# Tile 0's gate branch and projections first, tile 1's and the samples' between tile 0's expert rows

## The chip, the cores and the metric

One core of a Trainium2 chip runs the kernel. The metric is the device time of one execution in microseconds (us). TensorE (PE) multiplies matrices, VectorE (DVE), ScalarE (ACT) and GpSimd (POOL) do the rest, SyncE (SP) issues transfers, and 16 DMA engines move data between HBM and SBUF. PSUM, where TensorE writes, has 8 banks of 512 columns.

## The reference

One layer of a hybrid decoder over 256 prompt tokens and 8 sample tokens that share the weights, all in float32 with a model width D of 2048:

```python
h = rms_norm(x, norm1_w)
zb, zc, zx, zq, zk, zv, zmq, zg = jnp.split(h @ w_in, SPLIT_POINTS, axis=-1)
y_conv = (zb * short_conv(zc * zx)) @ w_conv_out
y_diff = rms_norm(diff_attn(q, k, v), subln_w) * (1 - lam_init) @ w_diff_out
y_mem  = mem_attn(qm, mem_k, mem_v) @ w_cross_out
g = sigmoid(zg.reshape(B, T, 3, D))
x = x + (g[:,:,0] * y_conv + g[:,:,1] * y_diff + g[:,:,2] * y_mem) @ w_o
# then experts: 8 heads, each token picks 16 of 16384 in every head
h2 = rms_norm(x, norm2_w);  q = (h2 @ w_peer_q).reshape(n, 8, 2, 128)
s1, s2 = q[:, :, 0] @ sub_keys[0].T, q[:, :, 1] @ sub_keys[1].T
idx, top_s = top_16_of_pair_sums(top_k(s1, 16), top_k(s2, 16))
a = einsum(take(peer_u, idx), h2);  w = softmax(top_s) * gelu(a)
x = x + einsum(w, take(peer_v, idx))
```

Every token reads 128 rows of `peer_u` and 128 of `peer_v`, each 8 KB, at places that only the scores tell.

## The kernel before

Tokens are three tiles: prompt tile 0 (128 tokens), prompt tile 1 (128) and the 8 samples, NT = 264 columns together. Activations lie turned, with features on the partitions: `hT` holds 16 blocks (KC) of 128 features by 264 tokens.

**Projections.** A weight matrix comes in blocks of 256 columns, [128, 16, 256] of float32, 2 MB, in runs of 1 KB, by SyncE into one of two buffers `wring[r]`. A block is two chunks. `chunk` (L569 to L574) adds 16 matmuls of a 128x128 piece of the weights (the stationary side) with 264 moving columns; each of these matmuls is two MATMUL and two LDWEIGHTS instructions in the trace. `linear` (L576) walks over the blocks. For w_o and w_peer_q a second step per chunk follows: `turner` (L589) turns w_o's chunk back to rows and VectorE adds it to x (L1256), `score` (L851) multiplies w_peer_q's chunk with the sub-keys. SyncE's `stream` fetches the next block into a buffer as soon as both chunks of the last one are done.

**Gate branches.** `gate_chunk` (L647) computes one unit: 16 matmuls for the gate's 128 columns (L651) and 8 for the branch's output (L663), whose weights come in 1 MB blocks to `bwring`, a part of `bregion`. ScalarE takes the sigmoid, VectorE multiplies and adds to `merged`. There are 48 units, q = 0 to 47, in three branches; the attention is threaded into the first 32 of them. The last 16 (`branch(2, ...)`, w_diff_out) stand alone.

**Experts.** Once the scores of a head are there, VectorE's `route` finds the 16 winners of each token and signals `idx_ready`. GpSimd then gathers: `gather_u` (one row of `peer_u` for each of 128 tokens, one indirect transfer of 1 MB) and `gather_v` (the same of `peer_v`). VectorE's `dot` (L1765) multiplies a gathered u row with `h2` and sums it. ScalarE makes a diagonal matrix of weights (L1150), and TensorE's `add_rows` (L878) adds diagonal x v row to four PSUM banks. A group g is one head of one tile, 16 slots: g 0 to 7 are tile 0's, g 8 to 15 tile 1's; the samples' 8 u rows are slots of their own inside g 7 and 8, and their v rows follow tile 0's. u rows have 4 buffers (`u_slots`), v rows 8 (`e_slots`). `v_before(n)` says how many v rows are gathered by u slot n: v follows u at a distance of 28 slots (`V_LEAD`).

**What sets the order.** Each engine runs its program in order and waits on counters. SyncE's stream, GpSimd's gathers, TensorE's program and VectorE's slots (`for g ... for j`, with `route_next` at j = 3) are written out by hand. GpSimd's gathers and SyncE's weights are two DMA queues that share the same 16 engines.

## Time and profile before

| | |
|---|---|
| median of 3 runs | 2857.49 us (2852.1 to 2860.66) |
| profiled execution | 2857.79 us, span 2855.9 us |
| TensorE busy | 2478.5 us (87%) |
| VectorE busy | 1390.6 us (49%) |
| ScalarE busy | 355.1 us (12%) |
| GpSimd busy | 1038.9 us (36%) |
| DMA, both queues | 913.67 MB, mean 320 GB/s |
| mean granted TensorE clock | 0.964 of full |

The profile is one execution. Busy times are shares of the whole span and hide that the stages have different limits, so a table by stretch is read beside them. The DMA share is the mean busy share of the 16 DMA engines. In a list in order of time, `[1.76 <-DVEq L1183]` after a row means that the engine stood idle for 1.76 us before it and what ended that.

### The profile page before, as it was taken

Reading aid. Unit: us, or ns where it says so; the run is one execution under the profiler, and the core shown is the slowest. Engines: PE = TensorE matmul, PEld = TensorE weight load, DVE = VectorE, ACT = ScalarE, POOL = GpSimd, SP = SyncE. Lnnn points to the kernel's source line nnn. Section 1 sums busy time; section 2 is a strip of 40 time slices with the busy share of each in tenths; the row PEclk is TensorE's granted clock in tenths of the full one; section 3 lists DMA queues with packets and bytes.
Section 4 is the critical chain, followed back from the end, with each engine's and each line's share of the span. In section 5 each row is a group of like instructions: output and inputs, shape, how many; then the busy total and the mean of one; then the engine's idle time right before and its main releaser. Section 6 shows DMA issues by size and latency. Waiting matters only on the chain.

```text
span 2855.9 us, 28287 instructions
## 1 busy us (share of the span) xinstructions
PE 2478.5 (87%) x9241; PEld 1592.3 (56%) x9241; DVE 1390.6 (49%) x2168; ACT 355.1 (12%) x760; POOL 1038.9 (36%) x952
## 2 busy tenths in 40 slices
...
GB/s 156 153 335 319 316 337 335 192 332 153 195 339 322 330 275 180 155 138 119 146 200 355 401 421 417 417 417 411 422 422 416 413 360 422 418 421 417 421 422 376
DMA packets 305393, 913.67 MB, mean 320 GB/s; under 512 B 15634, under 2 KB 195946, under 8 KB 236652
## 3 DMA queue, kind: packets, MB, share of 16 engines
q0 software_dynamic: 122304, 723.48, 63.0%
q1 hardware_dynamic: 182980, 188.92, 20.3%
...
HBM read 905.80 MB, written 6.56 MB: 319 GB/s over the span
## 4 chain that ended last, share of the span: by engine, by line
PE 53%; DMA 25%; DVE 12%; issue 5%; POOL 4%; ACT 1%; DVEq 0%; POOLq 0%; ACTq 0%; SPq 0%
PE ps L573 20%; PE ps L651 12%; DMA sb_S<-in_peer_u_dram,sb_ring 10%; DMA sb_bregion<-in_peer_u_dram,sb_ring 6%; PE ps L663 6%; PE ps L878 4%; DMA sb_mkv<-in_peer_u_dram,sb_ring 3%; PE ps L641 3%; PE ps L751 2%; DVE sb_bregion L1765 2%; DMA sb_wring<-in_w_in_dram 2%; DVE sb_S L1765 2%; DMA sb_S<-in_peer_v_dram,sb_ring 1%; POOL sb_bregion L486 1%; POOL sb_wring L486 1%
## 5 line engine op out<-in xcount | busy, mean ns | idle before, releaser
L878 PE MATMUL ps<-sb_wring,sb_ring 128*128 128x512 f32 x992 | 462.7, 617 | 129.7 <-DMA sb_wring<-in_peer_v_dram,sb_ring 80.8
L573 PE MATMUL ps<-sb_hT,sb_wring 128*128 128x264 f32 x2304 | 533.4, 393 | 18.2 <-DMA sb_wring<-in_w_peer_q_dram 8.7
L573 PEld LDWEIGHTS ps<-sb_hT,sb_wring 128*128 128x128 f32 x2304 | 442.2, 193 | 101.5 <-issue 23.1
L878 PEld LDWEIGHTS ps<-sb_wring,sb_ring 128*128 128x128 f32 x992 | 189.0, 197 | 404.2 <-issue 270.4
L1765 DVE CUSTOM_DVE_ANT_0 sb_bregion<-sb_bregion,sb_rows 128x2048 f32<-128x2048 f32 x128 | 293.6, 2294 | 228.7 <-DMA sb_bregion<-in_peer_u_dram,sb_ring 221.6
L651 PE MATMUL ps<-sb_hT,sb_wring 128*128 128x264 f32 x1536 | 365.8, 389 | 9.2 <-issue 6.8
L651 PEld LDWEIGHTS ps<-sb_hT,sb_wring 128*128 128x128 f32 x1536 | 286.5, 190 | 74.8 <-issue 27.7
L486 POOL DMA_INDIRECT sb_bregion<-in_peer_u_dram,sb_ring x132 | 187.2, 1419 | 280.2 <-DVEq L1183 228.0
L878 PE MATMUL ps<-sb_hT,sb_ring 128*128 128x512 f32 x496 | 234.9, 623 | 46.2 <-DMA sb_hT<-in_peer_v_dram,sb_ring 35.0
L878 PE MATMUL ps<-sb_oreg,sb_ring 128*128 128x512 f32 x496 | 223.4, 597 | 39.8 <-DMA sb_oreg<-in_peer_v_dram,sb_ring 37.2
L1150 ACT ACTIVATE sb_ring<-sb_ident,sb_ring 128x128 f32<-128x128 f32 x248 | 99.6, 402 | 909.5 <-PE ps L878 702.1
L1765 DVE CUSTOM_DVE_ANT_0 sb_S<-sb_S,sb_rows 128x2048 f32<-128x2048 f32 x64 | 146.7, 2292 | 107.1 <-DMA sb_S<-in_peer_u_dram,sb_ring 102.7
L1765 DVE CUSTOM_DVE_ANT_0 sb_mkv<-sb_mkv,sb_rows 128x2048 f32<-128x2048 f32 x64 | 146.7, 2292 | 105.2 <-DMA sb_mkv<-in_peer_u_dram,sb_ring 101.9
L878 PEld LDWEIGHTS ps<-sb_hT,sb_ring 128*128 128x128 f32 x496 | 95.4, 198 | 183.7 <-issue 134.7
L486 POOL DMA_INDIRECT sb_wring<-in_peer_v_dram,sb_ring x128 | 160.1, 1251 | 84.8 <-PE ps L878 43.6
L878 PEld LDWEIGHTS ps<-sb_oreg,sb_ring 128*128 128x128 f32 x496 | 91.5, 190 | 168.5 <-issue 148.6
L486 POOL DMA_INDIRECT sb_mkv<-in_peer_u_dram,sb_ring x66 | 101.6, 1540 | 135.6 <-DVEq L1183 120.0
L518 POOL COPY sb_ring<-sb_ring 128x16 int32<-128x16 int32 x16 | 17.2, 1077 | 346.1 <-DVEq L1183 346.0
L663 PE MATMUL ps<-sb_oreg,sb_bregion 128*128 128x264 f32 x512 | 122.1, 388 | 0.0
L573 PE MATMUL ps<-sb_conv,sb_wring 128*128 128x264 f32 x512 | 116.3, 387 | 2.1 <-DVEq L1183 1.8
L641 PE MATMUL ps<-sb_wring,sb_bregion 128*128 128x256 f32 x512 | 110.7, 379 | 0.0
L663 PEld LDWEIGHTS ps<-sb_oreg,sb_bregion 128*128 128x128 f32 x512 | 96.4, 190 | 25.4 <-issue 9.4
(349 smaller groups left out, 2530.2 us busy)
## 6 DMA issues: line engine op xcount, KB each, us to landing
sb_wring<-in_w_in_dram SPq DMA_DIRECT2D x52, 2048.0 KB, 13.3
...
sb_wring<-in_w_mem_kv_dram SPq DMA_DIRECT2D x8, 2048.0 KB, 8.8
sb_wring<-in_w_o_dram SPq DMA_DIRECT2D x8, 2048.0 KB, 8.1
sb_wring<-in_w_peer_q_dram SPq DMA_DIRECT2D x8, 2048.0 KB, 13.7
```

Of the source, the lines that this page charges most:

```text
L486: nc.gpsimd.indirect_dma_start(dst, None, table, bass.IndirectOffsetOnAxis(ap=idx, axis=0)).then_inc(landed, 16)
L518: st(nc.gpsimd.tensor_copy(uidx[:, g % 4, :], idx_flat[:, g * TOPK:(g + 1) * TOPK]))
L573: last = mm(ps[:, (2 * r + c) % 4, 0:NT], wring[:, r, k, c * P:(c + 1) * P], rhs[:, k, :], start=(k == 0), stop=(k == KC - 1))
L641: last = mm(ps[:, 2 * r + t, 0:BLK], memT[:, k, t * P:(t + 1) * P], wring[:, r, k, :], start=(k == 0), stop=(k == KC - 1))
L651: last = mm(ps[:, c, 0:NT], wring[:, r, k, c * P:(c + 1) * P], hT[:, k, :], start=(k == 0), stop=(k == KC - 1))
L663: last = mm(ps[:, 2, 0:NT], bwring[:, r, k, c * P:(c + 1) * P], operand[:, k, :], start=(k == 0), stop=(k == BC - 1))
L751: last = mm(ps[g * QUAD:g * QUAD + w.shape[1], 6 + q, :], w, v_slots[page_slot(p)][:, q * 512:(q + 1) * 512], start=first, stop=final)
L878: last = mm(ps[:, 4 * t + q, :], diag[:, k % 4, :], e_slots[v % ER][:, q * 512:(q + 1) * 512], start=False, stop=q_stop, skip_group_check= ...
L1150: st(A_(diag[:, k % 4, :], ident[:, :], ACT.Copy, scale=wexp[:, g % 4, j:j + 1]))
L1765: st(V.tensor_tensor_reduce(out=u_slots[n % UR], in0=u_slots[n % UR], in1=h2, scale=1.0, scalar=0.0, op0=ALU.mult, op1=ALU.add, accum_out= ...
```

## The change

The last gate branch (16 units), w_o (16 chunks), the norm and w_peer_q (16 chunks) are first done for tile 0's 128 columns alone. For tile 1 and the samples (`LATE`, 136 columns) the same steps are written between the slots of tile 0's experts, and their weights are fetched a second time.

- SyncE: after `stream(8, w_pq, ...)` it runs the branch's stream, w_o's and w_peer_q's again.
- TensorE, ScalarE and VectorE each have a `late_item(n)`, called at u slot n: gate units at n = 0, 2, ... 30 with their merge on VectorE two slots later, w_o chunks at n = 33, 35, ... 63, the norm at 67 to 74, w_peer_q chunks from 72 to 109, each on every second or third slot.
- TensorE's experts follow the slots: in slot n stand, behind the late item, the experts that `v_before` gives for n - 4.
- PSUM: tile 0's accumulators keep banks 0 to 3 and the late steps use banks 4 to 7.
- Buffers: while the late weights need `wring` and `bwring`, u rows have 3 buffers (4 from slot 128 on) and v rows 4 (9 from `V_WIDE` on, the v row that goes with slot 120).
- The samples' routes, dots and v rows move from heads 2 to 9 to heads 8 to 14. Tile 0's routes stand closer together: heads 1 to 7 are routed within slots 3 to 51 (before: one in each group).

```diff
-        u_slots = [bregion[:, 0:D], bregion[:, D:2 * D], mkv[:, 0, :], work]
-        e_slots = w_slots + [hflat[:, 0:D], hflat[:, D:2 * D], oflat[:, 0:D], oflat[:, D:2 * D]]
+        u_homes = [rows[:, 1, 0:D], rows[:, 1, D:2 * D], rows[:, 2, 0:D], mkv[:, 0, :]]
+        v_homes = [rows[:, 2, D:2 * D], oflat[:, 0:D], cflat[:, 0:D], work] + w_slots + [hflat[:, D:2 * D]]
...
-        OWN_ROUTED, OWN_HEAD = 5, 7
+        OWN_HEAD, OWN_V = 12, 14 * TOPK
-        V_LEAD, V_LEFT = 28, 12
+        V_LEAD, V_LEFT, V_LAG = 28, 12, 4
+        GATE_AT = {2 * i: i for i in range(16)}
+        MERGE_AT = {n + 2: i for n, i in GATE_AT.items()}
+        O_AT = {33 + 2 * m: m for m in range(17)}
+        ADD_AT = {n + 1: m - 1 for n, m in O_AT.items() if m}
+        NORM_AT = 67
+        PQ_AT = {(72 + 5 * m // 2 if m < 16 else 112): m for m in range(17)}
...
             stream(8, w_o, 0, C_O, ("y_full", 48))
             stream(8, w_pq, 0, C_PQ, ("chunk_full", C_PQ))
+            branch_stream(3)
+            sp.wait_ge(s["y_full"], 64)
+            sp.dma_start(XR[1], A["x_prompt"][0, P:2 * P, :]).then_inc(s["x_late"], 16)
+            sp.dma_start(XR[2][0:TS], A["x_sample"].rearrange("b t d -> (b t) d")).then_inc(s["x_late"], 16)
+            stream(8, w_o, 0, C_O2, ("y_full", 64))
+
+            sp.wait_ge(s["idx_ready"], PH)
+            sp.dma_start(n2_w[1], A["norm2_w"][0:1, :].to_broadcast([P, D])).then_inc(s["n2_again"], 16)
+            stream(8, w_pq, 0, C_PQ2, ("chunk_full", C_PQ2))
...
-            linear(G_O, 8, C_O, merged, turner(C_O, R_O))
+            linear(G_O, 8, C_O, merged, turner(C_O, R_O, TILES[0:1]), P)
...
-            linear(G_PQ, 8, C_PQ, hT, score)
+            linear(G_PQ, 8, C_PQ, hT, score, P)
...
+            def late_unit(i):
+
+                q, r, c, pair = UNITS + i, i // 2 % NR, i % 2, i // 4
+                if c == 0:
+                    pe.wait_ge(w_landed[r], 16 * (G_GATE2 // NR + pair + 1))
+                pe.wait_ge(s["gate_done"], q + 1)
+                for k in range(KC):
+                    last = mm(ps[:, 4 + c, 0:LN], wring[:, r, k, c * P:(c + 1) * P], hT[:, k, LATE], start=(k == 0), stop=(k == KC - 1))
+                last.then_inc(s["gate_full"], 1)
+                pe.wait_ge(s["y_taken"], q + 2)
+                if c == 0:
+                    pe.wait_ge(bw_landed[r], 16 * (12 + pair + 1))
+                for k in range(BC):
+                    last = mm(ps[:, 6, 0:LN], bwring[:, r, k, c * P:(c + 1) * P], oT_diff[:, k, LATE], start=(k == 0), stop=(k == BC - 1))
+                last.then_inc(s["y_full"], 1)
...
+            add_zero(0, True, False)
+            for n in range(U_SLOTS):
+                late_item(n)
+                for v in range(v_before(n - V_LAG), v_before(n + 1 - V_LAG)):
+                    expert(v)
+            for v in range(v_before(U_SLOTS - V_LAG), V_SLOTS):
+                expert(v)
...
+            def late_merge(i):
+
+                q = UNITS + i
+                dve.wait_ge(s["gate_done"], q + 3)
+                dve.wait_ge(s["y_full"], q + 1)
+                st(TT(zst[:, q % 2, 0:LN], zst[:, q % 2, 0:LN], ps[:, 6, 0:LN], ALU.mult))
+                st(TT(merged[:, i, LATE], merged[:, i, LATE], zst[:, q % 2, 0:LN], ALU.add))
+                signal("y_taken")
```

The order on TensorE around the end of w_peer_q and the first experts. L856 and L910 are the scores, L870 and L922 zero the accumulators, L878 and L930 are the experts, L953 and L959 a late gate unit, L969 a late w_o chunk, L977 its turn. Before:

```order
L856 MATMUL ps<-sb_mkv,sb_zst 128x128 x2
L856 MATMUL ps<-sb_mkv,sb_zst 8x128
L578 REGISTER_ALU
L578 COMPARE_AND_BRANCH
L870 MATMUL ps<-sb_ring 128x512 x4
L878 MATMUL ps<-sb_wring,sb_ring 128x512 x16
L878 MATMUL ps<-sb_hT,sb_ring 128x512 x8
L878 MATMUL ps<-sb_oreg,sb_ring 128x512 x8
```

Now, at the same place and, after the last of the 16 late gate units, at the first experts:

```order
L910 MATMUL ps<-sb_mkv,sb_zst 128x128
L633 REGISTER_ALU
L633 COMPARE_AND_BRANCH
L922 MATMUL ps<-sb_ring 128x512 x4
L953 MATMUL ps<-sb_hT,sb_wring 128x136 x16
L959 MATMUL ps<-sb_oreg,sb_bregion 128x136 x8
```

```order
L930 MATMUL ps<-sb_rows,sb_ring 128x512 x4
L930 MATMUL ps<-sb_oreg,sb_ring 128x512 x4
L969 MATMUL ps<-sb_conv,sb_wring 128x136 x16
L930 MATMUL ps<-sb_conv,sb_ring 128x512 x4
L930 MATMUL ps<-sb_S,sb_ring 128x512 x4
L969 MATMUL ps<-sb_conv,sb_wring 128x136 x16
L977 MATMUL ps<-sb_ident,sb_zst 128x128
L977 MATMUL ps<-sb_ident,sb_zst 8x128
```

Sixteen late gate units stand ahead of the first expert, and from slot 33 on one late chunk stands ahead of every two experts.

The order on VectorE at the end of the third u slot: L1966 is the dot, L1991 the second half of `late_merge`, L1878 begins the next routing. Before, four dots stood in a row and then the routing:

```order
L1765 ISA sb_bregion,sb_ring<-sb_bregion,sb_rows 128x2048
L1765 ISA sb_ring 128x1
L1765 ISA sb_bregion,sb_ring<-sb_bregion,sb_rows 128x2048
L1765 ISA sb_ring 128x1
L1765 ISA sb_mkv,sb_ring<-sb_mkv,sb_rows 128x2048
L1765 ISA sb_ring 128x1
```

Now:

```order
L1991 TENSOR_TENSOR sb_conv<-sb_conv,sb_zst 128x136
L1966 ISA sb_rows,sb_ring<-sb_rows 128x2048
L1966 ISA sb_ring 128x1
L1878 MAX sb_mkv<-sb_mkv 128x8 x2
L1881 MAX_INDEX sb_mkv<-sb_mkv 128x8
```

A merge, which waits for TensorE's late unit 0, stands between the third and the fourth dot.

The order on SyncE after tile 0's w_peer_q. Before, the outputs came next:

```order
L277 DMA sb_wring<-in_w_peer_q_dram 128x16x256
L285 REGISTER_ALU
L285 COMPARE_AND_BRANCH
L321 DMA out_y_prompt_dram<-sb_rows 128x2048
L323 DMA out_y_sample_dram<-sb_rows 8x2048
```

Now the late branch's blocks come next, and behind them those of w_o and w_peer_q:

```order
L312 DMA sb_wring<-in_w_peer_q_dram 128x16x256
L320 REGISTER_ALU
L320 COMPARE_AND_BRANCH
L312 DMA sb_wring<-in_w_in_dram 128x16x256
L334 DMA sb_bregion<-in_w_diff_out_dram 128x8x256
L312 DMA sb_wring<-in_w_in_dram 128x16x256
L334 DMA sb_bregion<-in_w_diff_out_dram 128x8x256
```

## Rows read from the trace of the kernel before

**Rows 1.** The page: busy times, GB/s by slice of 71 us, DMA queues.

```profile
PE 2478.5 (87%) x9241; PEld 1592.3 (56%) x9241; DVE 1390.6 (49%) x2168; ACT 355.1 (12%) x760; POOL 1038.9 (36%) x952
...
GB/s 156 153 335 319 316 337 335 192 332 153 195 339 322 330 275 180 155 138 119 146 200 355 401 421 417 417 417 411 422 422 416 413 360 422 418 421 417 421 422 376
...
q0 software_dynamic: 122304, 723.48, 63.0%
q1 hardware_dynamic: 182980, 188.92, 20.3%
```

**Rows 2.** Busy time by stretch; the last columns are granted clock, DMA share, GB/s.

```profile
1122.00:1294.00 172.00, 171.01 (x769) 145.70 (x767) 14.52 (x34) 6.26 (x16) 1.29 (x2) 1.00 0.49 159
1294.00:1434.00 140.00, 134.67 (x611) 109.19 (x612) 10.38 (x35) 15.86 (x34) 0.00 (x0) 0.95 0.42 135
...
1480.00:1570.00 90.00, 78.47 (x360) 64.78 (x359) 71.64 (x125) 8.30 (x27) 47.26 (x24) 0.94 0.95 362
...
1600.00:2300.00 700.00, 551.59 (x1168) 219.74 (x1169) 471.46 (x926) 79.61 (x167) 373.02 (x280) 0.92 1.01 417
2300.00:2350.00 50.00, 50.00 (x117) 21.98 (x117) 28.27 (x58) 7.26 (x17) 25.58 (x21) 0.99 0.85 347
```

**Rows 3.** TensorE in order of time: start, duration, line, shape, count.

```profile
1121.97 7.28 PE L651 MATMUL ps<-sb_hT,sb_wring 128*128 128x264 f32 x32
1129.09 3.72 PE L663 MATMUL ps<-sb_oreg,sb_bregion 128*128 128x264 f32 x16
1132.65 7.28 PE L651 MATMUL ps<-sb_hT,sb_wring 128*128 128x264 f32 x32
...
1294.77 14.50 PE L573 MATMUL ps<-sb_conv,sb_wring 128*128 128x264 f32 x64 [1.76 <-DVEq L1183]
...
1417.03 0.54 PE L594 MATMUL ps<-sb_ident,sb_zst 128*128 128x128 f32 x3 [0.35 <-ACTq L968]
1418.88 12.50 PE L558 MATMUL ps<-sb_ident,sb_rows 128*128 128x128 f32 x48 [1.31 <-DVEq L1183]
...
1433.61 16.24 PE L573 MATMUL ps<-sb_hT,sb_wring 128*128 128x264 f32 x64 [0.85 <-DVEq L1183]
```

**Rows 4.** TensorE with few moving columns, in time; then the weight loads' group.

```profile
1019.02 0.60 PE L710 MATMUL ps<-sb_ident,sb_ring 128*128 128x128 f32 x4
1069.01 1.84 PE L762 MATMUL ps<-sb_ones,sb_ring 128*128 128x1 f32 x16
...
L651 PEld LDWEIGHTS ps<-sb_hT,sb_wring 128*128 128x128 f32 x1536 | 286.5, 190 | 74.8 <-issue 27.7 <-DMA sb_wring<-in_w_in_dram 1.6
```

**Rows 5.** DMA in 1122 to 1294: GB/s by slice of 4.3 us; issues, us to landing.

```profile
GB/s 398 346 339 351 32 237 349 145 0 0 245 348 139 0 0 265 347 120 0 0 267 348 116 0 0 278 348 106 0 0 291 348 92 0 0 310 177 0 0 0
...
sb_wring<-in_w_in_dram SPq DMA_DIRECT2D x7, 2048.0 KB, 8.1
sb_bregion<-in_w_diff_out_dram SPq DMA_DIRECT2D x7, 1024.0 KB, 10.4
```

**Rows 6.** DMA issues of w_peer_q in 1294 to 1434, then in 1480 to 1600.

```profile
sb_wring<-in_w_peer_q_dram SPq DMA_DIRECT2D x2, 2048.0 KB, 8.4
...
sb_wring<-in_w_peer_q_dram SPq DMA_DIRECT2D x4, 2048.0 KB, 22.7
```

**Rows 7.** In time: first routing, first gather, first dot; VectorE's longest waits after 1600.

```profile
1459.93 0.49 DVE L1678 MAX8 sb_mkv<-sb_conv 128x8 f32<-128x128 f32 x2 [9.77 <-ACTq L983]
...
1470.95 1.03 POOL L486 DMA_INDIRECT sb_bregion<-in_peer_u_dram,sb_ring  x1 [0.95 <-POOL sb_ring L518]
...
1477.26 2.29 DVE L1765 CUSTOM_DVE_ANT_0 sb_bregion<-sb_bregion,sb_rows 128x2048 f32<-128x2048 f32 x1 [7.23 <-DMA sb_bregion<-in_peer_u_dram,sb_ring]
...
DVE sb_bregion L1765 <- DMA sb_bregion<-in_peer_u_dram,sb_ring: 208.3, 84, 11.9
```

**Rows 8.** Two experts in a clean stretch of the expert phase, in time.

```profile
1794.26 3.67 PE L878 MATMUL ps<-sb_wring,sb_ring 128*128 128x512 f32 x8 [1.31 <-DMA sb_wring<-in_peer_v_dram,sb_ring]
1799.21 3.67 PE L878 MATMUL ps<-sb_wring,sb_ring 128*128 128x512 f32 x8 [1.29 <-DMA sb_wring<-in_peer_v_dram,sb_ring]
```

More of the change, by code:

```diff
@@ L645, in _, with gate_chunk @@
             own_scores()
-            def gate_chunk(b, r, c, q, operand, landed, between=None, ready=None):
+            def gate_chunk(b, r, c, q, operand, landed, between=None, ready=None, width=NT):
                 pe.wait_ge(s["gate_done"], q + 1)
                 for k in range(KC):
-                    last = mm(ps[:, c, 0:NT], wring[:, r, k, c * P:(c + 1) * P], hT[:, k, :], start=(k == 0), stop=(k == KC - 1))
+                    last = mm(ps[:, c, 0:width], wring[:, r, k, c * P:(c + 1) * P], hT[:, k, 0:width], start=(k == 0), stop=(k == KC - 1))
                     if k == KC - 1:
@@ L854, in score @@
                 pe.wait_ge(s["rows_taken"], m + (R_PQ + 1))
-                for t, (first, n) in enumerate(TILES):
-                    last = mm(ps[0:n, 4 + q % 2, t * P:(t + 1) * P], zst[:, q % 2, first:first + n], skT[:, q % 2, :], start=True, stop=True)
-                last.then_inc(s["tr_full"], 1)
-            linear(G_PQ, 8, C_PQ, hT, score)
+                mm(ps[:, 4 + q % 2, 0:P], zst[:, q % 2, 0:P], skT[:, q % 2, :], start=True, stop=True).then_inc(s["tr_full"], 1)
+            linear(G_PQ, 8, C_PQ, hT, score, P)
             pe.wait_ge(s["rows_taken"], 64 + 2)
@@ new lines, in late_chunk, with late_turn @@
+            def late_chunk(m, g0, c0, rhs):
+                r, c, pair = m // 2 % NR, m % 2, m // 4
+                if c == 0:
+                    pe.wait_ge(w_landed[r], 16 * (g0 // NR + pair + 1))
+                pe.wait_ge(s["chunk_taken"], c0 + m + 3)
+                for k in range(KC):
+                    last = mm(ps[:, 4 + c, 0:LN], wring[:, r, k, c * P:(c + 1) * P], rhs[:, k, LATE], start=(k == 0), stop=(k == KC - 1))
+                last.then_inc(s["chunk_full"], 1)
+            def late_turn(m):
+                pe.wait_ge(s["chunk_taken"], C_O2 + 4 + m + 1)
+                pe.wait_ge(s["rows_taken"], R_O2 + m + 1)
+                for t, (first, n) in enumerate(LATE_TILES):
+                    last = nc.tensor.transpose(ps[0:n, 6 + m % 2, t * P:(t + 1) * P], zst[:, m % 2, first:first + n], ident[:, :])
+                last.then_inc(s["tr_full"], 1)
```

438 lines of the change are left out of this document (299 added, 139 removed).

## The prediction

> **What bounds the kernel now.** I read the share of busy time first [rows 1], then the table by stretch [rows 2], then the order of time inside single stretches. The shares alone mislead: TensorE is busy 87% of the span, but the table shows two regimes. Up to about 1470 us TensorE is full (171.01 of 172 us in the stretch of the last gate branch, granted clock 1.00) and the DMA engines half idle (share 0.49, then 0.42). From 1480 us on the DMA engines are full, with share 1.01 and 417 GB/s over 700 us, and TensorE has gaps (551.59 of 700). The expert phase is 264 u gathers and 264 v gathers of 128 rows by 8 KB, 1.0486 MB each, 553.6 MB in all: at the 421 GB/s of the page's full slices [rows 1] that is 1315 us, against the 1385 us from the first gather (1470.95) to the end of the span. So the time is the instant of the first gather plus the DMA work from there on. VectorE's dots wait for landings in this phase [rows 7], and experts in a clean stretch start 4.95 us apart for 3.67 us of work [rows 8], so neither is the bound.
>
> **What the change removes ahead of the first gather.** It narrows the moving side of the last gate branch, w_o and w_peer_q from 264 columns to 128. Each matmul here is two instructions in the trace.
> - Gate branch: a unit is 32 + 16 instructions, 10.68 us (1121.97 to 1132.65) [rows 3]: 222 ns for 264 columns. At 128 columns the nearest rows are four transposes in 0.60 us, and sixteen instructions that load 128x128 weights for a single column in 1.84 us [rows 4]. Both times hold the way of the last one through the array, so the twelve further instructions took 1.24 us, 103 ns each: a weight load can be had every 103 to 110 ns. I take 110 ns, a unit of 5.3 us, 16 units 85 instead of 171 us: **-86 us**. Weights: a block (2 units) is 3.15 MB; the gate part lands 8.1 us after its issue and the branch part 10.4 [rows 5], and the buffer is wanted 10.6 us later. It fits, narrowly.
> - w_o: 16 chunks in 122.8 us (1294.77 to 1417.57) [rows 3]. At 110 ns a chunk is 3.5 us, with turn and the wait at the loop's end 4.1. A block then takes 8.1 us, exactly its landing time of 8.1 [rows 5]. 8 x 8.2 = 66: **-57 us**. Upper end of its cost: 8.7 a block, +4.
> - Transposes and norm: 12.50 us of ScalarE-paced transposes [rows 3] with narrower copies, about 10.5: **-2**. From the start of the w_peer_q stage (1433.61) to the first gather (1470.95) are 37.3 us, of which about 26 are the three chunks and two scores ahead of the first routing [rows 3, 7]. The chunks fall to half, the routing of about 10 us stays: **-13**.
> In sum the first gather moves from 1471 to about 1313 us: **-158 us**.
>
> **What it adds to the DMA engines.** The late part reads 8 gate blocks, 8 w_diff_out blocks, 8 w_o blocks and 8 w_peer_q blocks again: 24 x 2.097 + 8 x 1.049 = 58.7 MB, in 1 KB packets. The price: queue 1 moved 188.92 MB in 20.3% of 16 engines' span, 580 us, so 3.07 us a MB, or 180 us for the late weights; in bursts with weights alone it reached 348 GB/s [rows 1, 5], which gives 168. In the one stretch that mixed them with gathers (1480 to 1570) the share was 0.95 and 362 GB/s [rows 2], no sign that the two kinds share engines for free. Since gathers fill the engines up to the end, all of it is on the path. I take the burst's price, since here too a queue always has its next packets waiting: **+168 us**. Two further loads (tile 1's x, norm2 weights, 1 MB each) cost +5, and about one w_peer_q block more has landed before the first gather, -9: **-4**.
>
> The Trainium skill speaks against this price: DMA: Bandwidth & Descriptors, section Specifications, asks for at least 512 B a transfer for line rate, and its section Bandwidth measures 425 GB/s in a large copy. By that rule 1 KB packets cost no more than gathers, 58.7 MB would be an estimated 138 us and the sum 30 us lower. The rows disagree: 188.92 MB of such packets took 3.07 us a MB [rows 1], and 417 GB/s is 2.40. The measurement decides.
>
> **What of the stalls changes.** Before, of the 1385 us 1315 are gathers, 30 the rest of w_peer_q (some 10.5 MB at 348 GB/s) and 5 outputs. That leaves about 35: 6 until the first u row lands, 8 more up to 1600 (VectorE routes, four u buffers), 8 in 2300 to 2350 (share 0.85, where tile 1's experts wait for the samples' output), 6 at the end and 7 of stretches just under the full rate [rows 2, 7]. The late weights fill the second, and the third goes, since the samples' rows move to heads 12 to 14 and tile 1's accumulators (banks 4 to 7) no longer wait for them: about 20 are left. New ones:
> - VectorE's third u slot is followed by the merge of late unit 0, which can't come before TensorE has finished tile 0's 16 scores (1288 + 16 x 3.9 plus waits for contended weights, some 1355) and unit 0. So dots and u gathers stop from about 1329 to 1360; queued behind that merge are all further dots, then GpSimd. What hides it: between 1313 and 1360 the DMA engines have six u rows, about three w_peer_q blocks and the first late gate block to move, 15 + 18 + 9 = 42 of the 47 us. Not hidden, with their uneven order: some 8 us.
> - Gate phase, slots 2 to 32: 4 slots need 4 u rows (10 us) and 3.15 MB of weights (9 us), 19 us of DMA; VectorE 4 dots of 2.5, 2 merges of about 0.9 and 0.6 of a routing, 18 us. Near enough to leak: 8 us.
> - w_o and w_peer_q phases, slots 33 to 112: TensorE must give 3.7 us an expert [rows 8] and one late chunk of 32 instructions at 136 columns, about 115 ns each, with its turn 4.3 us, each 2 slots: 6.0 us a slot against the DMA's 6.6 (5.0 for u and v, 1.5 for weights). TensorE does not bind, but a chunk stands ahead of experts, v has 4 buffers for 8 before and u 3 for 4, and late w_o's first block is only issued once the last late unit is done. In flight stay up to 7 rows of 2.5 us, 17 us of cover for a stall of about 8. I put 12 us.
> So 20 + 28 = 48 against 35, rounded to **+12 us**.
>
> **Sum.** -158 + 168 - 4 + 12 = +18 us. Against the profiled run's 2857.79 (span 2855.9, which stands 0.3 above the median) that is 2876, as a median 2875.
>
> **Rivals.**
> 1. *The head start just pays* (same). If the two queues overlap a little better or half the new stalls stay under the row queue, 14 of the 28 us go: 2861; with the lower bound for w_o too, 2857. For it: share 1.01 through nearly every stretch after 1600 although VectorE stops 10 us at each routing. Against: fewer buffers now. Chance 0.23, 2849 to 2866.
> 2. *The weights are cheap in company* (faster). If 1 KB packets beside 8 KB rows cost only what their bytes do at 417 GB/s, 141 instead of 168 us: 2848; with few new stalls 2835. For it: the skill's rule above. Against: rows 1 and the mixed stretch. Chance 0.13.
> 3. *TensorE's in-order stream takes the bound* (slower than forecast). Experts stand behind late chunks that wait for weights; a w_peer_q block took 22.7 us to land against 8.4 without gathers [rows 6], as two queues share the engines. A late block is wanted every 4 slots. If each waits so that v's four buffers are all landed and u stands behind v on GpSimd, the engines run empty. It decides from about 0.93 of full DMA share in slots 33 to 112 (some 500 us): 35 instead of 12, with the gate phase as bad: 2905 to 2915. At the granted clock of 0.92 of 1600 to 2300 [rows 2] TensorE's 6.0 us a slot would be some 6.3, still under 6.6. Chance 0.16.
> 4. *It doesn't do what it says*: the first gather does not come earlier since narrow matmuls are held by their weight loads (190 ns each [rows 4]), a chunk 6.1 us: branch 146, w_o 107, so the first gather some 102 us later than forecast, time 2977. The sixteen loads in 1.84 us of the same rows speak plainly against it. Chance 0.02.
>
> **Numbers.** Forecast case (2866 to 2900) 0.46, rival 1 0.23, rival 2 0.13, rival 3 0.16, rival 4 0.02. Range 2843 to 2912: it leaves out the low half of rival 2, the upper part of rival 3 and rival 4. A measurement of this kernel tells 0.3% (8.6 us) from no change: faster (below 2849) 0.13, same 0.23, slower 0.64.
>
> **What would show it.** First gather near 1313 us (1290 to 1330). Late branch units of the first pass 5.3 us apart, w_o chunks near 4.1. From the first gather to slot 112 GB/s of 370 to 400 with share near 1.0, queue 1 at about 248 MB in all and 3 us a MB. Wrong would be: first-pass units above 6 us (rival 4 or a weight bound); share below 0.95 with TensorE waiting for late weights (rival 3); queue 1 below 2.6 us a MB (rival 2). Where the end of the span minus the first gather is not 1560 +- 30 us, the second half of the sum is wrong.

## The result and the profile after

The changed kernel is slower by 2.6%: 2930.73 us (median of 4 runs, 2925.74 to 2933.9) against 2855.31 of the kernel before beside it, a ratio of 1.026 with an interval of 1.0237 to 1.0285. The sign was forecast, the size was not: 2875 was predicted, and 2912 was the upper end.

The page of the kernel after: the span, GB/s by slice of 73 us, and the DMA queues (packets, MB, share of 16 engines).

```profile
span 2923.9 us, 32344 instructions
...
GB/s 153 172 336 321 316 340 298 219 308 127 275 333 323 330 188 276 259 213 300 348 371 352 396 390 387 411 374 403 415 411 403 394 383 419 421 419 418 324 422 376
...
q0 software_dynamic: 122144, 722.36, 61.9%
q1 hardware_dynamic: 241140, 249.80, 26.1%
```

Against [rows 1] queue 1 moved 60.9 MB more (249.80 - 188.92), and its packets took 26.1% of 2923.9 us instead of 20.3% of 2855.9: 763 - 580 = 183 us more. Queue 0 moved the same rows and took 1810 instead of 1799 us. 400 GB/s is first reached in the 26th slice and held from the 34th on but for one slice and the last; the kernel before reaches it in the 23rd and holds it but for one and the last.

**The head start came.** In order of time, TensorE's narrow units, its w_o stage and its w_peer_q stage, then GpSimd's first gather (start, duration, line, shape, count, wait):

```profile
1134.88 3.74 PE L706 MATMUL ps<-sb_hT,sb_wring 128*128 128x128 f32 x32
1140.24 1.95 PE L706 MATMUL ps<-sb_hT,sb_wring 128*128 128x128 f32 x16
...
1206.20 7.41 PE L628 MATMUL ps<-sb_conv,sb_wring 128*128 128x128 f32 x64 [1.48 <-DVEq L1386]
...
1282.92 3.35 PE L628 MATMUL ps<-sb_hT,sb_wring 128*128 128x128 f32 x14 [0.85 <-DVEq L1386]
...
1308.42 1.03 POOL L534 DMA_INDIRECT sb_rows<-in_peer_u_dram,sb_ring  x1 [0.92 <-POOL sb_ring L572]
```

A unit takes 5.36 us (1134.88 to 1140.24) where it took 10.68 [rows 3]. The first gather is at 1308.42 instead of 1470.95 [rows 7]: 163 us earlier. By stage the branch took 83 us less (1116.61 to 1206.20, before 1121.97 to 1294.77), w_o 57 (65.8 for 122.8), the transposes and the norm 5 (10.9 for 16.0), and the start of w_peer_q up to the gather 12 (25.5 for 37.3). That is 157; the other 5 lie ahead of the first narrow unit, where the two kernels do the same work. They are a difference between executions: in the trace of `e3_weigh`, equal up to there, that unit begins at 1123.14.

**What came behind it.** From the first gather to the end of the span it took 1616 us, against 1385 before. Both kernels, cut at the same u slots (0, 3, 33, 66, 113, 160, 200, 232, 263, end), busy time by engine; the last columns are granted clock, DMA share and GB/s. After:

```profile
1308.00:1376.00 68.00, 55.01 (x433) 51.80 (x432) 7.94 (x9) 9.54 (x27) 7.71 (x6) 0.92 0.91 309
1376.00:1537.00 161.00, 104.02 (x725) 98.02 (x723) 115.05 (x249) 13.73 (x29) 51.95 (x37) 0.83 0.97 350
1537.00:1772.00 235.00, 194.56 (x824) 123.88 (x824) 112.34 (x220) 24.79 (x59) 81.66 (x71) 0.91 0.98 381
1772.00:2062.00 290.00, 258.81 (x1004) 151.46 (x1005) 114.96 (x110) 52.16 (x132) 119.78 (x99) 0.93 1.00 394
2062.00:2318.00 256.00, 189.29 (x406) 76.80 (x404) 197.07 (x450) 25.54 (x55) 128.79 (x100) 0.95 0.98 404
2318.00:2525.00 207.00, 157.12 (x323) 64.21 (x324) 141.46 (x289) 24.88 (x54) 109.81 (x82) 0.89 0.99 406
2525.00:2687.00 162.00, 147.46 (x313) 61.77 (x312) 82.98 (x106) 19.11 (x41) 85.05 (x71) 0.89 1.01 419
2687.00:2860.00 173.00, 127.57 (x285) 48.38 (x284) 84.14 (x109) 14.90 (x32) 72.31 (x66) 0.88 0.92 381
2860.00:2924.00 64.00, 50.73 (x116) 21.28 (x114) 24.45 (x17) 5.83 (x15) 12.23 (x13) 0.97 0.89 369
```

The kernel before, at the same slots:

```profile
1471.00:1485.00 14.00, 14.00 (x67) 11.74 (x66) 7.18 (x7) 0.39 (x1) 8.08 (x6) 1.00 1.04 400
1485.00:1608.00 123.00, 88.54 (x396) 70.74 (x397) 87.77 (x141) 16.58 (x45) 68.44 (x42) 0.89 0.95 368
1608.00:1777.00 169.00, 141.42 (x305) 58.45 (x304) 132.23 (x303) 24.49 (x50) 98.88 (x67) 0.96 1.01 419
1777.00:2017.00 240.00, 175.08 (x374) 69.49 (x373) 175.27 (x379) 28.54 (x60) 141.47 (x102) 0.96 1.01 416
2017.00:2257.00 240.00, 227.64 (x483) 88.89 (x482) 137.57 (x221) 25.34 (x54) 112.79 (x95) 0.93 1.01 419
2257.00:2473.00 216.00, 152.34 (x338) 62.87 (x337) 116.32 (x166) 23.14 (x49) 105.54 (x89) 0.91 0.97 398
2473.00:2636.00 163.00, 123.14 (x267) 49.07 (x266) 93.55 (x149) 19.79 (x43) 85.67 (x69) 0.98 1.01 419
2636.00:2793.00 157.00, 118.47 (x257) 48.50 (x256) 81.65 (x108) 17.36 (x38) 70.94 (x65) 0.95 1.01 421
2793.00:2856.00 63.00, 50.33 (x115) 21.06 (x113) 24.21 (x17) 5.04 (x13) 13.17 (x14) 0.98 0.89 369
```

Row by row the lead of 163 us shrinks. At slot 3 it is 109 us (1376 against 1485), at slot 33 71, at slot 66 5; at slot 113 the changed kernel is 45 us behind, at slot 263 67. A full stretch shows a share of 1.01, so a stretch's idle time is its length times (1 - share/1.01). Summed, that is some 58 us after and some 23 before. With the packets' own durations, which the shares round, I get 60 and 23, and use these below. The level of 1.01 is a choice, good to a few us in either sum; the difference of 37 hardly moves with it. The books of the stretch behind the first gather are then: **+194 us of DMA work, +37 us of idle DMA engines**, against a head start of 163: +68 us, the profiled runs' 2925.74 - 2857.79.

Two places make the idle time visible. VectorE at slots 2 and 3, in time:

```profile
1321.80 2.29 DVE L1966 CUSTOM_DVE_ANT_0 sb_rows<-sb_rows 128x2048 f32<-128x2048 f32 x1 [0.68 <-DMA sb_rows<-in_peer_u_dram,sb_ring]
...
1374.74 0.29 DVE L1990 TENSOR_TENSOR sb_zst<-sb_zst,ps 128x136 f32<-128x136 f32 x1 [50.63 <-PE ps L959]
```

The third dot is followed by the merge of late unit 0 and 50.63 us without a dot, while the share of this stretch is still 0.91. And TensorE between the experts of heads 12 and 13:

```profile
2687.47 6.17 PE L930 MATMUL ps<-sb_wring,sb_ring 128*128 128x512 f32 x14
2725.86 4.73 PE L930 MATMUL ps<-sb_hT,sb_ring 128*128 128x512 f32 x7 [32.21 <-ACTq L1296]
```

TensorE waits 32.21 us for a diagonal (L1296). VectorE computes the weights of head 13 (`weigh(13)`, 2724.63 to 2725.3) only behind slot 6 of group 14, behind a routing. Meanwhile the v buffers are full and the gathers run dry: the share of the stretch of slots 232 to 263 is 0.92.

### The profile page after: what moved, and what is told of

It is laid out like the page before. It is cut to its first block, busy times and chain, and to the rows that moved or that the text cites. A ratio compares the mean times of both kernels' runs of the same rounds, so it can differ in the third digit from the quotient of the medians.

```text
span 2923.9 us, 32344 instructions
## 1 busy us (share of the span) xinstructions
PE 2506.9 (86%) x11033; PEld 1695.0 (58%) x11033; DVE 1399.4 (48%) x2218; ACT 374.2 (13%) x844; POOL 1001.9 (34%) x951
## 3 DMA queue, kind: packets, MB, share of 16 engines
q1 hardware_dynamic: 241140, 249.80, 26.1%
## 4 chain that ended last, share of the span: by engine, by line
PE 51%; DMA 26%; DVE 14%; issue 4%; POOL 2%; ACT 1%; another core or an unknown queue 0%; DVEq 0%; ACTq 0%; POOLq 0%; SPq 0%
PE ps L628 16%; DMA sb_rows<-in_peer_u_dram,sb_ring 11%; PE ps L706 10%; PE ps L930 8%; DVE sb_rows L1966 5%; PE ps L718 5%; DMA sb_wring<-in_w_o_dram 4%; DMA sb_wring<-in_w_peer_q_dram 4%; PE ps L969 3%; PE ps L696 3%; PE ps L806 2%; DMA sb_mkv<-in_peer_u_dram,sb_ring 2%; DMA sb_rows<-in_peer_v_dram,sb_ring 2%; DMA sb_wring<-in_w_in_dram 2%; DVE sb_mkv L1966 1%
## 5 line engine op out<-in xcount | busy, mean ns | idle before, releaser
L628 PE MATMUL ps<-sb_hT,sb_wring 128*128 128x264 f32 (+1 forms) x2304 | 474.2, 368 | 16.9 <-DMA sb_wring<-in_w_peer_q_dram 9.6
L1966 DVE CUSTOM_DVE_ANT_0 sb_rows<-sb_rows 128x2048 f32<-128x2048 f32 x128 | 293.7, 2294 | 366.3 <-DMA sb_rows<-in_peer_u_dram,sb_ring 361.0
L534 POOL DMA_INDIRECT sb_rows<-in_peer_u_dram,sb_ring x230 | 284.7, 1238 | 480.9 <-DVEq L1386 407.4
L930 PE MATMUL ps<-sb_wring,sb_ring 128*128 128x512 f32 x552 | 264.1, 632 | 65.2 <-DMA sb_wring<-in_peer_v_dram,sb_ring 39.8
L706 PE MATMUL ps<-sb_hT,sb_wring 128*128 128x264 f32 (+1 forms) x1536 | 309.2, 352 | 11.0 <-issue 6.8
L1966 DVE CUSTOM_DVE_ANT_0 sb_rows<-sb_rows,sb_bregion 128x2048 f32<-128x2048 f32 x96 | 220.1, 2293 | 176.0 <-DMA sb_rows<-in_peer_u_dram,sb_ring 170.1
L930 PEld LDWEIGHTS ps<-sb_wring,sb_ring 128*128 128x128 f32 x552 | 109.1, 203 | 219.3 <-issue 166.3
L930 PE MATMUL ps<-sb_oreg,sb_ring 128*128 128x512 f32 x328 | 155.8, 619 | 27.9 <-ACTq L1296 19.4
L930 PE MATMUL ps<-sb_rows,sb_ring 128*128 128x512 f32 x328 | 150.5, 602 | 13.2 <-DMA sb_rows<-in_peer_v_dram,sb_ring 9.8
L930 PE MATMUL ps<-sb_conv,sb_ring 128*128 128x512 f32 x320 | 146.6, 601 | 8.3 <-DMA sb_conv<-in_peer_v_dram,sb_ring 8.3
L930 PE MATMUL ps<-sb_S,sb_ring 128*128 128x512 f32 x320 | 145.1, 596 | 7.7 <-DMA sb_S<-in_peer_v_dram,sb_ring 7.5
L930 PEld LDWEIGHTS ps<-sb_oreg,sb_ring 128*128 128x128 f32 x328 | 63.5, 198 | 113.0 <-issue 85.3
L930 PEld LDWEIGHTS ps<-sb_rows,sb_ring 128*128 128x128 f32 x328 | 61.0, 192 | 91.1 <-issue 76.3
L930 PEld LDWEIGHTS ps<-sb_conv,sb_ring 128*128 128x128 f32 x320 | 59.8, 192 | 84.1 <-issue 79.7
L930 PEld LDWEIGHTS ps<-sb_S,sb_ring 128*128 128x128 f32 x320 | 59.5, 190 | 84.1 <-issue 81.9
L930 PE MATMUL ps<-sb_hT,sb_ring 128*128 128x512 f32 x136 | 66.2, 633 | 48.7 <-ACTq L1296 41.1
L696 PEld LDWEIGHTS ps<-sb_wring,sb_bregion 128*128 128x128 f32 x512 | 97.3, 190 | 13.2
L969 PE MATMUL ps<-sb_conv,sb_wring 128*128 128x136 f32 x512 | 70.6, 302 | 38.2 <-DMA sb_wring<-in_w_o_dram 20.6
```

The source lines that it names most:

```text
L534: nc.gpsimd.indirect_dma_start(dst, None, table, bass.IndirectOffsetOnAxis(ap=idx, axis=0)).then_inc(landed, 16)
L628: last = mm(ps[:, (2 * r + c) % 4, 0:width], wring[:, r, k, c * P:(c + 1) * P], rhs[:, k, 0:width], start=(k == 0), stop=(k == KC - 1))
L696: last = mm(ps[:, 2 * r + t, 0:BLK], memT[:, k, t * P:(t + 1) * P], wring[:, r, k, :], start=(k == 0), stop=(k == KC - 1))
L706: last = mm(ps[:, c, 0:width], wring[:, r, k, c * P:(c + 1) * P], hT[:, k, 0:width], start=(k == 0), stop=(k == KC - 1))
L930: last = mm(ps[:, 4 * t + q, :], diag[:, k % 4, :], v_homes[v_at[v]][:, q * 512:(q + 1) * 512], start=False, stop=q_stop, skip_group_check ...
L969: last = mm(ps[:, 4 + c, 0:LN], wring[:, r, k, c * P:(c + 1) * P], rhs[:, k, LATE], start=(k == 0), stop=(k == KC - 1))
```

## The experiments

All stand beside the kernel before on the same chip; intervals are those of the ratio. The kernel before took between 2852.54 and 2855.31 us in all of them, so times of different runs compare to some 3 us. Theory A is mine, B the rival, in the words on record.

**Do the re-read bytes cost what was forecast?** `e1_tiny` keeps every late fetch, wait and matmul, but a fetch brings one block of 128 rows of the weight instead of 16 (or 8):

```diff
-    sp.dma_start(wring[:, r], src[:, :, ds(col, BLK)]).then_inc(w_landed[r], 16)
+    n = 1 if late[0] else KC
+    sp.dma_start(wring[:, r, 0:n], src[:, 0:n, ds(col, BLK)]).then_inc(w_landed[r], 16)
```

> The changed kernel, whose late weight fetches bring only one of the 16 row blocks (one of 8 for the branch weights): 3.7 MB instead of 58.7, all waits and matmuls as they are; it leaves out that part of the weights' data. Theory A (the engines' time for the late weights is what the change pays): 55 MB at the 3.05 us a MB of the changed kernel's queue 1 go, 168 us, less some 10 to 20 that VectorE and TensorE then hold back: 2765 to 2785 us. Theory B (the price is TensorE's in-order stream and the shallower buffers, and the bytes are mostly hidden): above 2850 us.

Measured: 2841.95 us against 2852.54, ratio 0.996 (0.9948 to 0.9974). Neither number: 55 of the 58.7 MB went and took 89 us with them (2930.73 - 2841.95), about half of what they occupy (55 x 3.01 = 166). The stretches up to slots 3, 33 and 66:

```profile
1307.00:1375.00 68.00, 54.64 (x432) 51.42 (x431) 7.97 (x9) 9.55 (x27) 7.76 (x6) 0.92 0.65 224
1375.00:1529.00 154.00, 108.89 (x762) 101.86 (x762) 115.42 (x250) 14.42 (x31) 54.01 (x37) 0.83 0.69 251
1529.00:1718.00 189.00, 179.07 (x787) 111.14 (x785) 111.87 (x220) 24.10 (x57) 93.91 (x71) 0.98 0.97 384
```

The first 33 slots take 222 us without the bytes and 229 with them, at a DMA share of 0.65 and 0.69. The same slots took 137 us before. So there a second chain is as long as the DMA's. Its first part, 68 us instead of 14, is TensorE's: tile 0's scores and late unit 0 stand ahead of the fourth dot. In its second part, 154 us instead of 123, VectorE has 30 dots, 16 merges and four routings (115.42 us busy), and 27.3 of the rest are waits for u rows. Two waits of slots 3 to 33 (total, times, longest), and two pieces of the chain that ended last:

```profile
POOL sb_rows L539 <- DVEq L1391: 133.4, 17, 52.7
DVE sb_rows L1971 <- DMA sb_rows<-in_peer_u_dram,sb_ring: 27.3, 13, 6.0
```

```profile
1441.84 8.45 DMA sb_rows<-in_peer_u_dram,sb_ring
1450.32 2.29 DVE sb_rows L1971
```

GpSimd waits for VectorE to free a buffer, the row lands some 8 us after its issue, and VectorE waits for it, while the DMA engines are a third idle. u rows have three buffers here and four before. What the missing fourth cost was not tested by itself: `e8_whole`, below, has four, the same routings and no merges, and takes 136 us for these slots. Only past slot 33 do the bytes cost their time: 189 us for slots 33 to 66 instead of 235. Of the head start of 163 us, 85 are therefore lost in the first 33 slots even when the weights are nearly free, and at the end 11 are left (2852.54 - 2841.95).

**Is it the bytes or the 1 KB runs?** `e2_long` fetches as many bytes in runs of 16 KB (8 KB for the branch's part). They come from other data, the same 2 MB of `peer_u` each time (`runs`), so the place changes with the length:

```diff
-    sp.dma_start(wring[:, r], src[:, :, ds(col, BLK)]).then_inc(w_landed[r], 16)
+    sp.dma_start(wring[:, r].rearrange("p k n -> p (k n)"), runs).then_inc(w_landed[r], 16)
```

> The changed kernel, whose late weight fetches bring as many bytes, but from whole rows of another tensor, in runs of 16 KB and 8 KB instead of 1 KB; it leaves out the right weights. Theory A (a 1 KB packet costs more of an engine than its bytes): the late 58.7 MB cost 2.4 us a MB as gathers do instead of 3.05, 38 us less: 2890 to 2895 us. Theory B (bytes alone count, or the late weights are not on the path): unchanged, 2925 to 2935 us.

Measured: 2906.31 us, ratio 1.0186 (1.0169 to 1.0203), 24 us less than the changed kernel. Its queue 1 (span 2908.7 us), and its stretch of slots 3 to 33:

```profile
q1 hardware_dynamic: 187892, 249.80, 24.9%
```

```profile
1379.00:1554.00 175.00, 114.33 (x763) 107.61 (x762) 115.60 (x250) 14.41 (x31) 52.57 (x37) 0.80 0.88 341
```

Queue 1's 60.9 extra MB cost 724 - 580 = 144 us instead of 183, so 2.4 us a MB against 3.01. That the length does it and not the place was not separated, but the gathers' 8 KB rows, which lie scattered, cost 2.4 too. The Trainium skill's rule, quoted in the prediction from DMA: Bandwidth & Descriptors, section Specifications, would have both at one price; these rows contradict it for 1 KB. Of the 39 us saved 24 came out in the median and 15 in the profiled execution; the rest turned into idle time, above all in slots 3 to 33, which took 175 us instead of 161 at a share of 0.88. VectorE waits 47.8 us for u rows there (11 times, at most 14.1), in the changed kernel 27.9 (13 times, at most 6.7): the buffer rounds of the first experiment, and longer ones.

**The hole at head 13.** `e3_weigh` moves two small steps of VectorE forward:

```diff
-                    if j == 6 and g >= 2:
+                    if j == (2 if g in (13, 14) else 6) and g >= 2:
                         weigh(g - 1)
```

> The changed kernel with the weights of heads 12 and 13 worked out at the third instead of the seventh slot of the next group. In the changed kernel TensorE idles 32 us up to 2725 us until VectorE has these weights, and the DMA engines are empty from 2725 to 2743. Theory A (that hole is lost time and comes from the samples' move): 4 slots of 6 are won, 12 to 18 us, 2913 to 2919 us. Theory B (the DMA work is only put off and later catches up): unchanged, 2926 to 2935.

Measured: 2922.87 us, ratio 1.0247 (1.023 to 1.0264), between the two. The stretch of slots 232 to 263 is here 158 us long instead of 173, and full:

```profile
2706.00:2864.00 158.00, 124.00 (x272) 45.81 (x271) 84.14 (x109) 15.08 (x33) 74.93 (x67) 0.92 1.01 421
```

So the hole is shown, with its cause, to be 15 us long in the trace. In the time it is not shown as clearly: the medians moved by 8, the intervals of the two ratios overlap, and the profiled execution itself took 2929.8 us, 4 more than that of the changed kernel. There the first gather is 6 us later (1314.88) and slots 33 to 66 take 11 us more (246 for 235). The edit touches only what stands behind slot 208, so both are differences between executions.

**The samples' routes.** `e4_routes` spreads them:

```diff
-        OWN_ROUTES = {(8, 6): 0, (8, 9): 1, (8, 13): 2, (9, 6): 3, (9, 9): 4, (9, 13): 5, (10, 6): 6, (10, 9): 7}
+        OWN_ROUTES = {(7, 9): 0, (7, 13): 1, (8, 9): 2, (8, 13): 3, (9, 9): 4, (9, 13): 5, (10, 6): 6, (10, 9): 7}
```

> The changed kernel with the samples' eight routes two to a group in groups 7 to 10, instead of three, three and two in groups 8 to 10. A group of 16 slots with four routes keeps VectorE 16 x 2.5 + 4 x 10.2 = 81 us, as long as the DMA engines need for its rows. Theory A (VectorE is the bound there and the holes of 2200 to 2400 us come from it): 8 to 12 us less, 2919 to 2923 us. Theory B (the holes come from elsewhere): unchanged within 4 us of 2930.

Measured: 2933.67 us, ratio 1.0279 (1.0252 to 1.0306): no gain, as B says, but not for B's reason. Slots 119 to 144 and 144 to 163:

```profile
2105.00:2241.00 136.00, 94.13 (x195) 37.19 (x193) 103.75 (x244) 12.91 (x27) 77.86 (x55) 0.93 0.98 400
2241.00:2340.00 99.00, 79.03 (x170) 33.56 (x171) 74.44 (x158) 14.04 (x30) 59.15 (x42) 0.90 1.01 414
```

The second stretch, with one route fewer, became full; the changed kernel has 0.98 in it and takes 100 us. The first got worse, 136 us at 0.98 for 134 at 0.99: the routes that moved to group 7 fall where u rows still have three buffers (up to slot 128). The stretch of slots 160 to 200, with two samples' routes and a prompt head's in group 10, kept its idle time. So the holes seem to have moved with the routes, by 1 to 2 us, which one execution of each hardly shows. In this kernel there is hardly a better place, since the samples' norm is done at slot 114 and their routes are wanted before head 12.

**VectorE's halt behind the third dot.** `e5_gate` starts the late units at slot 8 instead of 0 and gives one every 1.5 slots:

```diff
-        GATE_AT = {2 * i: i for i in range(16)}
+        GATE_AT = {8 + 3 * i // 2: i for i in range(16)}
```

> The changed kernel with the 16 late gate units at slots 8 to 30 (every one and a half slots) instead of 0 to 30, so that VectorE's first merge stands behind ten dots and not three. Theory A (VectorE's halt from 1324 to 1375 us, in which the gathers stop, is lost DMA time): the 15 us idle of 1310 to 1540 us go for the most part, 2915 to 2922 us. Theory B (the weights of the first pass and of the first late units use the engines meanwhile, so the halt costs little): 2925 to 2935 us.

Measured: 2928.87 us, ratio 1.0254 (1.0234 to 1.0274): within the runs of the changed kernel, as B says. The stretches up to slots 3, 33 and 66:

```profile
1306.00:1323.00 17.00, 9.55 (x84) 9.17 (x82) 6.90 (x7) 1.94 (x7) 7.12 (x6) 0.90 0.93 346
1323.00:1532.00 209.00, 149.20 (x1064) 139.86 (x1064) 116.04 (x251) 21.33 (x49) 50.84 (x38) 0.87 0.95 343
1532.00:1781.00 249.00, 192.32 (x824) 123.23 (x824) 112.79 (x220) 24.78 (x59) 83.27 (x71) 0.88 0.95 365
```

Slot 3 begins 53 us earlier (1323 against 1376), slot 33 5 us earlier, and slot 66 later. A 50 us wait, the largest of its kind in the trace, was worth nothing: now TensorE waits in slots 3 to 33 for late weights instead, 23.2 us for gate blocks and 11.2 for w_diff_out's, against 2.5 for gate blocks in the changed kernel.

**Does TensorE bind?** `e6_half` runs 8 of the 16 (4 of the 8) matmuls of each late unit and chunk, with the full fetches:

```diff
-                for k in range(KC):
-                    last = mm(ps[:, 4 + c, 0:LN], ..., start=(k == 0), stop=(k == KC - 1))
+                for k in range(8):
+                    last = mm(ps[:, 4 + c, 0:LN], ..., start=(k == 0), stop=(k == 7))
```

> The changed kernel with half the matmuls in each late unit and chunk (8 of 16 row blocks, 4 of 8 in the branch part), the weights fetched in full; it leaves out that half of the sums. TensorE's late work falls from about 200 to 100 us. Theory A (the DMA engines' work sets the pace, TensorE's in-order stream costs little): 5 to 12 us less, 2918 to 2926 us. Theory B (experts standing behind late chunks are what the bytes do not explain): 35 to 60 us less, 2870 to 2895 us.

Measured: 2938.56 us, ratio 1.0295 (1.0276 to 1.0315): nothing gained, so TensorE's late matmuls are not on the path. Its waits for late weights remain in this run. Slots 3 to 33 and 33 to 66:

```profile
1369.00:1530.00 161.00, 75.66 (x367) 66.53 (x366) 115.72 (x250) 13.71 (x29) 54.59 (x37) 0.68 0.98 354
1530.00:1774.00 244.00, 171.08 (x568) 97.00 (x568) 111.71 (x219) 24.76 (x59) 80.57 (x71) 0.84 0.95 368
```

**How much do the lent buffers cost?** `e7_v3` takes one more of them away:

```diff
-        v_at, v_use, v_earlier = homes_of(V_SLOTS, 4, len(v_homes), V_WIDE)
+        v_at, v_use, v_earlier = homes_of(V_SLOTS, 3, len(v_homes), V_WIDE)
```

> The changed kernel with 3 instead of 4 buffers for v rows while the late weights run. Theory A (in 1390 to 2060 us rows in flight cover the stalls): up to 8 us more, 2928 to 2938 us. Theory B (the shallow buffers let the engines run empty, and 8 to 4 buffers was a cost of the change): 25 us or more on top, above 2955 us.

Measured: 2948.2 us, ratio 1.0337 (1.0306 to 1.0369), 17 us more, between the two. Slots 3 to 33 and 33 to 66:

```profile
1372.00:1540.00 168.00, 104.71 (x726) 98.43 (x725) 115.21 (x249) 13.72 (x29) 48.64 (x35) 0.81 0.94 338
1540.00:1783.00 243.00, 197.30 (x824) 124.17 (x824) 112.06 (x219) 24.76 (x59) 83.12 (x71) 0.91 0.94 367
```

The shares fall from 0.97 and 0.98 to 0.94. Buffers matter; that the step from eight to four cost little is read from those shares and was not tested, nor was u's step from four to three.

**The split against everything else.** `e8_whole` keeps the changed kernel's new order (experts by slots, the samples in heads 12 to 14, early routes) with the early `weigh` of `e3_weigh`, and u rows have four buffers and v rows eight throughout; it runs the last branch, w_o and w_peer_q once, with all 264 columns:

```diff
-            linear(G_O, 8, C_O, merged, turner(C_O, R_O, TILES[0:1]), P)
+            linear(G_O, 8, C_O, merged, turner(C_O, R_O))
...
-            linear(G_PQ, 8, C_PQ, hT, score, P)
+            linear(G_PQ, 8, C_PQ, hT, score)
...
             for n in range(U_SLOTS):
-                late_item(n)
```

> Everything of the change but its core: the last gate branch and both projections are done for all 264 columns at once, weights read once, and there are no late items; kept are the samples' move to heads 12 to 14, tile 0's early routes, TensorE's order by slots and the separate homes (4 buffers for u, 8 for v), with the earlier weights of heads 12 and 13 of the run before. Theory A (the samples' move does what I forecast: tile 1's experts do not wait for the samples' output): the 8 us hole of 2300 to 2350 goes, 2843 to 2850 us against 2855. Theory B (order and move cost time of their own, 8 to 20 us of what the split was blamed for): 2860 to 2875 us.

Measured: 2871.97 us, ratio 1.0061 (1.0045 to 1.0077). Without the split, the double reading and the fewer buffers, and with the early `weigh`, 59 of the 75 us are gone. `e3_weigh` has that `weigh` too and is 51 us slower, so 51 belong to the split and what it needs, and by the medians some 8 to the late `weigh`. The new order around them has 17 more of its own. Slots 3 to 33, 113 to 160, and 160 to 200:

```profile
1484.00:1620.00 136.00, 104.04 (x430) 76.76 (x430) 106.68 (x219) 22.27 (x65) 70.89 (x41) 0.92 0.88 334
2028.00:2283.00 255.00, 192.18 (x410) 78.22 (x408) 197.00 (x451) 26.14 (x56) 125.11 (x98) 0.93 0.98 403
2283.00:2490.00 207.00, 154.64 (x316) 62.42 (x317) 140.91 (x289) 24.64 (x52) 110.74 (x81) 0.90 0.99 407
```

**Can the rest be had back?** `e9_spread` is `e8_whole` with the routes apart:

```diff
-            ROUTE_AT = {(0, 3): 1, (0, 9): 2, (1, 3): 3, (1, 9): 4, (2, 3): 5, (2, 9): 6, (3, 3): 7}
-            ROUTE_AT.update({(g - 1, 3): g for g in range(PH, 2 * PH)})
+            ROUTE_AT = {(g - 1, 3): g for g in range(1, 2 * PH)}
-        OWN_ROUTES = {(8, 6): 0, (8, 9): 1, (8, 13): 2, (9, 6): 3, (9, 9): 4, (9, 13): 5, (10, 6): 6, (10, 9): 7}
+        OWN_ROUTES = {(g, j): 2 * (g - 6) + j // 13 for g in range(6, 10) for j in (9, 13)}
```

> The whole-width kernel of e8_whole (all of the change but the split of tile 0 from tile 1 and the samples; nothing is read twice), with one edit: tile 0's heads are routed one in a group of 16 slots, as in the kernel before, and the samples' eight routes two in a group over groups 6 to 9 instead of eight in groups 8 to 10. Theory A: the 0.6% that e8_whole lost to the kernel before is VectorE's crowded routing; from the first gather to slot 33 the DMA engines were idle for 17.6 us there against 7.5 in the kernel before, and 6.5 more around slots 113 to 160. With the routes spread both go back to some 7 and 1, idle in all from 34.8 to about 18, and since the hole of the kernel before at 2300 to 2350 us (9.4 us idle) does not come back, the time is 2848 to 2857, 0 to 0.3% under the kernel before. Theory B: what e8_whole lost is the new order itself (experts a fixed four slots behind, buffers in other places), not the routing: 2864 to 2876, as e8_whole.

Measured: 2849.33 us against 2854.46, ratio 0.9989 (0.9978 to 0.9999), as A says. The same stretches, of which the last two are now full:

```profile
1484.00:1608.00 124.00, 107.62 (x431) 79.17 (x430) 88.39 (x143) 22.22 (x65) 70.39 (x41) 0.94 0.96 368
2016.00:2263.00 247.00, 192.89 (x416) 80.09 (x416) 197.57 (x451) 27.59 (x60) 143.39 (x102) 0.94 1.01 416
2263.00:2465.00 202.00, 156.12 (x325) 63.64 (x326) 122.73 (x213) 24.77 (x53) 105.94 (x82) 0.90 1.01 417
```

Idle time fell from 35 to 13 us and the time by 23. The stretch of slots 160 to 200, which before held a hole (216 us at a share of 0.97), takes 202 us at 1.01. So crowded routing was what the new order lost, and the samples' place behind head 13 does close the hole of the kernel before. Against the kernel before the gain is 0.1%, less than the 0.3% that counts as a difference here: this version is level with it, the best of those that compute the whole layer, and it reads nothing twice.

## Why the prediction was right or wrong

- **Head start, -158: right.** 163 us, of which 157 lie in the stages that were forecast: 83 for 86, 57 for 57, 5 for 2 and 12 for 13. The price of a narrow matmul, read from sixteen loads in 1.84 us [rows 4], gave a unit of 5.3 us; it took 5.36.
- **Weights, +168: a step that failed in its size.** That the re-read bytes are paid in full at a 1 KB price was right. Queue 1's packets took 183 us more, of which the forecast had 173 (168 and 5 for the two further loads). The burst's 348 GB/s was the lower of my two prices; the mean over the queue, 3.07 us a MB, was nearer to the measured 3.01.
- **The block that "has landed before the first gather", -9: wrong.** Behind the first gather queue 1 moved 71.4 MB, before 11.6: 59.8 of the 60.9 extra MB, so the credit was 1 MB, some 3 us. TensorE's narrow stage read its weights faster, but the routing began after the same number of chunks, with the same blocks outstanding: 12 w_peer_q blocks are issued behind the first gather, eight of them late ones, and before there were four [rows 6].
- **What the forecast didn't have:** the gathers' own packets got slower. Queue 0's time rose by 11 us for the same gathers. Why is open: company of the 1 KB packets is not it alone, since in `e1_tiny`, with 3.7 MB of late weights, queue 0 took still longer, 64.2% of 2839.4 us or 1823 us, and the gathers' 8 KB packets 322 ns in the mean. With the two points above it is +30 of DMA work (10 + 9 + 11; the 3 us of credit are within the rounding).
- **Stalls up to slot 112: right in sum, partly for other reasons.** Idle there, with the wait for the first row, were 25 us; 34 were forecast (6 + 8 + 8 + 12). VectorE's halt was 51 us long for 31 forecast: tile 0's last score ended near 1365 instead of 1355, and zeroing the accumulators (3.70 us) and the whole of unit 0 came behind it. Yet the cover held, and `e5_gate` shows that the halt was free. Rival 3 asked for a share under 0.93 in slots 33 to 112; it was 0.98 and 1.00, although a late w_peer_q block took some 43 us to land (the median of the six issued in 1772 to 2062), and TensorE waited for late weights:

```profile
PE ps L969 <- DMA sb_wring<-in_w_peer_q_dram: 22.2, 3, 14.0
PE ps L969 <- DMA sb_wring<-in_w_o_dram: 20.6, 4, 9.4
PE ps L969 <- issue: 17.6, 1, 17.6
```

  That is 60 us of waiting in 525 (line, what was waited for, total, times, longest), while the DMA engines stood idle for some 10 in all. `e6_half` excludes TensorE's late matmuls from the other side, though not its waits.
- **Stalls past slot 112: the step that failed most.** The term of +12 for stalls measured 37. I let the hole of 2300 to 2350 [rows 2] go and set nothing in its place: 13 us forecast, 36 measured. That hole did go. But I moved the samples in thought only as far as the accumulators. With their rows behind head 13, v rows of heads 8 to 13 run eight v slots nearer to their u rows, while `weigh` stayed at slot 6: 15 us (`e3_weigh`). And their routes fell into groups 8 to 10, where up to four routings of 10.2 us and 16 dots of 2.48 us make 81 us for VectorE's 16 slots against the DMA's 80: some 11 us in slots 113 to 200. `e8_whole` has 10 there and `e9_spread` none, with the split away; inside the split kernel spreading them gained nothing (`e4_routes`), so its share there is shown only in part.
- **The stalls of the kernel before** were mis-sized too: 35 us, where the reckoning that gives 60 after gives 23. The gathers had been priced at the rate of the page's fullest slices, 1315 us, and their packets took 1340, at a share of 1.01 some 1327. So of the idle term's miss of 25, some 12 lie before the change and some 13 behind it (61 for the 47 forecast), of which the two points above are -9 and +23.
- **Sum.** Forecast +18; DMA work +30, idle +25, head start -5: +68. The prediction's own sign had said it: the end of the span minus the first gather came out at 1616 us, outside 1560 +- 30.
- **The deeper miss** is one that the sum could hide. It adds stalls of a few us to a sum of bytes, and so expects cheaper bytes to shorten the time in full. `e1_tiny` shows that the first 33 slots had a second chain, of TensorE's scores and late unit 0, VectorE's merges and routings and the three u buffers, of 222 us against 137 before. Even with nearly no late weights the change had only 11 us to give; rival 2's condition, weights at the gathers' price (chance 0.13), was met in `e2_long`, and it still was 1.9% slower.
